# Ten slots instead of eight for the gathered expert rows of a two-layer trunk, in the room of two kept tiles

## The reference, cut to what matters

```python
for i in range(2):
    h = h + token_mixer(rms_norm(h, ...))          # three kinds of attention, then y @ w_o[i]
    h = h + peer_ffn(rms_norm(h, ...))             # product-key experts
    h = h + per_layer_embedding(h, p[i], ...)      # sigmoid(norm(h) @ w_ple_gate) * (p_i @ w_ple)
return rms_norm(h, final_norm_g)

def peer_ffn(h):                                   # for each token
    scores = queries x sub_keys                    # 8 heads, two halves, 128 keys
    s1, i1 = top_k(scores half 0, 16); s2, i2 = top_k(scores half 1, 16)
    top_s, top_j = top_k(s1 + s2, 16); ids = i1 * 128 + i2 at top_j
    act = softmax(top_s) * gelu(expert_u[ids] . x)
    out = sum over heads and k of act * expert_v[ids]
```

## Time and profile before

| what | value |
|---|---|
| median of 3 runs | 1553.22 us (1552.20 to 1555.97) |
| the profiled execution, own time | 1551.98 us |
| its span, first to last instruction | 1550.2 us |
| mean granted TensorE clock | 0.803 of full speed |
| read from HBM | 605.09 MB, 391 GB/s over the span |

### The profile page before, as it was taken

The page is one execution under the profiler, slowest core; times in us unless marked ns, Lnnn a source line. Parts: engine busy times, 40 slices in busy tenths (PEclk is TensorE's granted clock), DMA queues, the critical chain, the costliest instruction groups (busy, mean ns, idle before and its releaser), DMA issues.

```text
span 1550.2 us, 18373 instructions
## 1 busy us (share of the span) xinstructions
PE 1140.1 (74%) x6360; PEld 446.3 (29%) x6360; DVE 1071.2 (69%) x2731; ACT 574.1 (37%) x1800; POOL 577.8 (37%) x516
## 2 busy tenths in 40 slices
PE   9987676895558865688657887698565866777666
PEld 6754133351113522235112343245011311111112
DVE  3489996579997245567998536757799664454455
ACT  0514456333343135423334325733234443333332
POOL 0023544445443232435453323434344343333330
PEclk9999788987779976789678897889657986656668
DMA  9178999999999999999999999999999999999993
GB/s 360 61 286 343 417 411 402 375 412 422 420 411 417 418 416 419 420 418 397 422 421 418 420 418 414 398 390 419 419 421 422 400 422 421 422 421 422 421 421 117
DMA packets 90254, 607.36 MB, mean 392 GB/s; under 512 B 9904, under 2 KB 10416, under 8 KB 24624
## 3 DMA queue, kind: packets, MB, share of 16 engines
q0 software_dynamic: 73728, 536.90, 84.1%
q1 hardware_dynamic: 16272, 69.02, 11.2%
q10 hardware_dynamic: 160, 0.26, 0.1%
HBM read 605.09 MB, written 1.05 MB: 391 GB/s over the span
## 4 chain that ended last, share of the span: by engine, by line
DVE 32%; DMA 31%; PE 26%; ACT 5%; issue 4%; POOL 2%; DVEq 0%; POOLq 0%; ACTq 0%
DMA ring<-in_rows,ids 31%; DVE ring L1272 14%; PE acc L572 8%; PE bank L868 2%; PE bank L724 2%; PE bank L605 2%; POOL ring L539 2%; DVE wb L1567 2%; PE bank L950 2%; PE bank L640 1%; DVE top_i L1561 1%; DVE y L1640 1%; PE bank L610 1%; DVE top_i L1576 1%; DVE y L1576 1%
## 5 line engine op out<-in xcount | busy, mean ns | idle before, releaser
L539 POOL DMA_INDIRECT ring<-in_rows,ids x512 | 577.6, 1128 | 931.8 <-PE acc L572 769.0
L572 PE MATMUL acc<-ring,diag 64*64 64x512 f32 x3968 | 682.0, 797 | 320.3 <-ACT diag L1038 316.1
L1272 DVE CUSTOM_DVE_ANT_0 ring<-ring,xc 128x1024 f32<-128x1024 f32 x504 | 606.6, 1224 | 359.0 <-DMA ring<-in_rows,ids 352.9
L1029 ACT ACTIVATE gel<-pre 128x1 f32<-128x1 f32 x512 | 103.3, 202 | 792.0 <-DVE pre L1272 765.7
L572 PEld LDWEIGHTS acc<-ring,diag 64*64 64x64 f32 x3968 | 139.5, 160 | 807.2 <-ACT diag L1038 690.3
L1038 ACT ACTIVATE diag<-cst,act_w 128x64 f32<-128x64 f32 x512 | 178.0, 348 | 17.1
L1035 ACT ACTIVATE act_w<-gate,gel 128x1 f32<-128x1 f32 x512 | 150.7, 294 | 17.1
L724 PE MATMUL bank<-wring,hT 128*128 128x512 f32 x96 | 47.1, 636 | 4.8 <-DVE hT L1309 4.1
L868 PE MATMUL bank<-hT,held 128*128 128x128 f32 x384 | 46.1, 278 | 3.1 <-DVE hT L1306 3.1
L868 PEld LDWEIGHTS bank<-hT,held 128*128 128x128 f32 x384 | 43.8, 192 | 13.0 <-issue 7.3
L1272 DVE DVE_READ_ACCUMULATOR2_ANT pre<- 128x1 f32 x512 | 41.7, 81 | 0.0
(11 more groups left out here) (278 smaller groups left out, 1103.1 us busy)
## 6 DMA issues: line engine op xcount, KB each, us to landing
wring<-in_w_in SPq DMA_DIRECT2D x16, 978.0 KB
wring<-in_w_out SPq DMA_DIRECT2D x12, 1024.0 KB
wring<-in_w_gate SPq DMA_DIRECT2D x11, 1024.0 KB
held<-in_w_query SPq DMA_DIRECT2D x8, 1024.0 KB, 16.3
ring<-in_rows,ids POOLq DMA_INDIRECT x512
ring<-in_w_in SPq DMA_DIRECT2D x8, 978.0 KB, 14.3
held<-in_w_out SPq DMA_DIRECT2D x2, 1024.0 KB, 12.1
held_latent<-in_w_latent SPq DMA_DIRECT2D x2, 768.0 KB
```

Source lines behind the costliest of these rows:

```text
L539: pool.indirect_dma_start(out=ring[:, n % RING, :], out_offset=None, in_=rows, in_offset=bass.IndirectOffsetOnAxis(ap=index, axis=0),).the ...
L572: last = pe.matmul(acc[rows_of(c), r, :], diag[rows_of(r), j, :], ring[rows_of(r), j, D:][:, cols_of(c)], start=False, stop=True, skip_gro ...
L1029: act.activation(gel[:, j:j + 1], pre[:, j:j + 1], ACT.Gelu).then_inc(gelued, 1)
L1272: dve.tensor_tensor_reduce(out=u, in0=u, in1=x, scale=1.0, scalar=0.0, op0=ALU.mult, op1=ALU.add, accum_out=pre[:, j:j + 1]).then_inc(dott ...
```

## The change

`ring` gets ten slots. The 16 KB per partition for the two new ones come from two places. `held` has four slabs: slab 3 of `w_o` goes through `wring` in every step, so it is loaded four times, not twice. `lifts` is gone: layer 0's product p @ `w_ple` is made at the start of `embed` as in layer 1, from `w_ple` that passes through `wring` once per tile, and DVE reads it in PSUM. A small tile `p0` holds one tile's half of p, and is loaded twice. The lists of the top keys are kept for two heads at a time, not for eight.

```diff
-RING = 8
+RING = 10
-HELD = KT // 2 + 1
+HELD = KT // 2
-OUT_HELD = KT // 2 - 1
-REST_LOADS = [("out", k) for k in range(OUT_HELD)]
+REST_LOADS = [("out", k) for k in range(KT // 2)]
 def weight_order():
-    order = [(kind, k, 0) for kind, k in REST_LOADS] + [("ple", 0, 0)]
+    order = [(kind, k, 0) for kind, k in REST_LOADS]
     for w in range(STEPS):
         if w >= 1:
+            order += [("ple", 0, w - 1)] if w <= TILES else []
             order += [(kind, k, w - 1) for kind, k in EMBED_LOADS
...
-        lifts = sb("lifts", [P, TILES, D])
+        p0 = sb("p0", [P, 2, P])
-        top_v = sb("top_v", [P, 2 * PH, TOPK])
-        top_i = sb("top_i", [P, 2 * PH, TOPK], U32)
+        top_v = sb("top_v", [P, 4, TOPK])
+        top_i = sb("top_i", [P, 4, TOPK], U32)
...
                 if n == WRING:
-                    load(slab(HELD - 1), source["out"](0, OUT_HELD), held_in[HELD - 1])
-                    for i in range(HELD - 1):
+                    for i in range(HELD):
                         load(slab(i), source["query"](0, i), held_in[i])
                     load(held_keys[:], source["keys"](0, 0), held_keys_in)
-                    load_p(0)
+                    load_p0(0)
+                if (kind, k, s) == ("gate", 2, 0):
+                    load_p0(1)
...
                 if (kind, k, s) == ("out", 0, TILES):
-                    load(slab(HELD - 1), source["out"](1, OUT_HELD), held_in[HELD - 1])
...
                 if n < RING:
-                    pool.wait_ge(slab_used, n + 1)
+                    pool.wait_ge(slab_used, min(n + 1, KT))
...
             def project_out(s, k):
-                kept = k == OUT_HELD
-                w = held[:, HELD - 1, :] if kept else weights()
+                w = weights()
...
-                    if kept:
+                    if k == KT // 2 - 1 and c == 0:
                         last.then_inc(out_half, 1)
-                if not kept:
-                    release(last)
+                release(last)
...
             def rest(s, turn):          # PE
                 if s == 1:
-                    next_of(lift_copied, 2)
...
             def choose(s, c, turn):     # PE
-                    if (s, c, i) == (0, 2, 4):
-                        pe.wait_ge(pT_in[0], 16)
-                        products(0, 0, weights(), bank[2:4]).then_inc(lift_made, 1)
-                    if (s, c, i) == (0, 3, 3):
-                        next_of(lift_copied, 2)
-                        release(products(0, 1, weights(), bank[2:4]))
...
             def lift(s):                # PE, at the start of embed
                 if l == 0:
+                    next_of(pT_in[0], 16)
+                    release(products(p0, weights()))
                     return
...
             def choose(s, c, turn):     # ACT
-                if (s, c) in ((0, 2), (0, 3)):
-                    for half in range(2):
-                        act.activation(lifts[:, c - 2, half * 512:(half + 1) * 512], bank[2 + half][:, :],
-                                       ACT.Copy).then_inc(lift_copied, 1)
...
                     for c in range(2):  # DVE, rest
-                        if i == 2:
+                        if i == 2 and c == 0:
                             next_of(out_half)
+                        if i == 2 and c == 1:
+                            wait_products(dve, "out", s, KT // 2 - 1)
...
-                    link(dve.tensor_tensor(g, g, made, ALU.mult))
+                    link(dve.tensor_tensor(g, g, bank[4 + c][:, :], ALU.mult))
```

More of the change, by code:

```diff
@@ L275, in trunk @@
         best_i = part_i[:, 1]
-        pT = (lifts[:, 1, 0:2 * SEQ].rearrange("p (a s) -> p a s", a=2), kTf[:])
+        p1 = kTf[:]
         hT_next = xc[:, 1, :].rearrange("p (k c) -> p k c", k=KT)
-        xc_tail = (xc[:, 0, :], lifts[:, 0, :])
-        gain_tail = lifts[:, 1, 0:512]
+        xc_tail = (xc[:, 0, :], held[:, 2, 0:D])
+        gain_tail = held[:, 2, D:D + 512]
         h_tail = wa[:, 0:1024].rearrange("p (r n) -> p r n", r=2)
@@ L325, in trunk @@
         lift_read = sem("lift_read")
-        lift_made = sem("lift_made")
-        lift_copied = sem("lift_copied")
         latent_done = sem("latent_done")
@@ L467, in slab, with load_p0 @@
                 return held[:, i, :].rearrange("p (a n) -> p a n", a=2)
-            def load_p(l):
-                load(pT[l], p_t[l * 2 * P:(l + 1) * 2 * P, :].rearrange("(a p) s -> p a s", p=P), pT_in[l])
+            def load_p0(t):
+                load(p0[:], p_t[0:2 * P, t * P:(t + 1) * P].rearrange("(a p) s -> p a s", p=P), pT_in[0])
             for n, (kind, k, s) in enumerate(order):
@@ L493, in _ @@
                 if (kind, k, s) == ("out", 2, TILES):
-                    for i in range(2, HELD - 1):
+                    for i in range(2, HELD):
                         load(slab(i), source["query"](1, i), held_in[i])
@@ L498, in _ @@
                     sp.wait_ge(query_ready, len(CHUNKS[0]) + 2 * (STEPS - 1))
-                    load_p(1)
+                    load(p1, p_t[2 * P:4 * P, :].rearrange("(a p) s -> p a s", p=P), pT_in[1])
                     load(slab(0), source["ple"](l, 0), held_in[0])
@@ L715, in project_out @@
                 l, t = layer_tile(s)
-                kept = k == OUT_HELD
-                if kept and t == 0:
-                    next_of(held_in[HELD - 1], 16)
-                w = held[:, HELD - 1, :] if kept else weights()
+                w = weights()
                 g = min(k, 2)
@@ L886, in rest, with products @@
                 turn()
-            def products(l, t, w, b):
+            def products(p, w):
                 for c in range(2):
                     for k in range(2):
-                        last = pe.matmul(b[c][:, :], pT[l][:, k, t * P:(t + 1) * P],
+                        last = pe.matmul(bank[4 + c][:, :], p[:, k, :],
                                          w[:, k * D + c * 512:k * D + c * 512 + 512], start=(k == 0), stop=(k == 1))
@@ L926, in lift @@
                     pe.wait_ge(pT_in[1], 16)
-                if s < STEPS - 1:
-                    products(l, t, held[:, 0, :], bank[4:6])
+                    products(p1[:, :, 0:P], held[:, 0, :])
                     return
@@ L934, in lift @@
                         for c in range(2):
-                            pe.matmul(bank[4 + r][rows_of(c), :], pT[l][:, k, tokens],
+                            pe.matmul(bank[4 + r][rows_of(c), :], p1[:, k, tokens],
                                       held[:, 0, :][:, k * D + c * 512:k * D + c * 512 + 512],
@@ L945, in embed @@
                 turn()
-                if l == DEPTH - 1 and s < STEPS - 1:
+                if s < STEPS - 1:
                     lift(s)
@@ L1583, in keys_top8 @@
                     next_of(keys_half)
-                top8(range(2 * a, 2 * z), top_v, top_i, lambda i: score(i, s))
+                first = 2 * a % 4
+                top8(range(first, first + 2 * (z - a)), top_v, top_i, lambda i: score(2 * a - first + i, s))
             def keys_next8(s, c):
+                a, z = CHUNKS[s][c]
+                first = 2 * a % 4
                 def spare(i):
-                    return wb[:, (2 * work_slot(i // 2, s) + i % 2) * P:(2 * work_slot(i // 2, s) + i % 2 + 1) * P]
-                a, z = CHUNKS[s][c]
-                next8(range(2 * a, 2 * z), top_v, top_i, lambda i: score(i, s), spare, s == 0)
+                    n = 2 * work_slot(a + (i - first) // 2, s) + i % 2
+                    return wb[:, n * P:(n + 1) * P]
+                next8(range(first, first + 2 * (z - a)), top_v, top_i, lambda i: score(2 * a - first + i, s), spare, s == 0)
             def choose(s, c, turn):
@@ L1603, in choose @@
                 turn()
-                halves = slice(2 * h0, 2 * (h0 + n))
+                halves = slice(2 * h0 % 4, 2 * h0 % 4 + 2 * n)
                 link(dve.tensor_copy(top_f[:, halves], top_i[:, halves]))
```

## The result

The changed kernel takes 1563.19 us (median of 5 runs, 1561.82 to 1567.07) against 1553.22. The ratio of the runs is 1.0061, 95% interval 1.0045 to 1.0076: 9.5 us slower, 7.0 to 11.8. The forecast was 5 us faster, with a range that ended at 1560.

What follows compares the result with a forecast made beforehand. The kernel was taken as bound by bytes at a 421 GB/s plateau. Slots -18.3, reloads +7.5 and start +5.5 gave -5.3 us against 1551.98: 1546.7, and 1548 for the runs' median, range 1540 to 1560.

Steps and rivals of the forecast that it cites:

- What two more slots give: Between first and last rows, two more slots keep the DMA engines running 5.0 us longer per stall: 18.3 us won.
- the first stall: 124 to 160 us, 7.7 us lost; two rows lying ready before the wait at 224.8 us win back 5.0.
- Reloads, 7.5 us: Three more slabs, two of `w_o` and one of `w_ple`, 3.15 MB in the bound stretch: 7.5 us lost, from 5.
- The start, 5.5 us, bounds 4.4 and 8.0: Step 0: slab 3 lands at 87.0 us behind queries, keys and p; PE waits, first rows come 5.5 us late.
- The reloads' landing in later steps: Slab 3 after step 0: a slab takes 7.3 us, 12.8 us are available in step 1, so cost nothing.
- the embedding product: Moved to the start of `embed` of steps 0 and 1, about 3.7 us each, covered by the deeper ring: 0.
- the text had said would make it wrong: Signs against the prediction: the plateau moves, stalls keep their size, or PE waits for `wring` after the start.
- The third, depth unused: Rival: stalls end with the compute engines, only some 6 us won of 13.0 lost; 7 us slower, 1560; chance 0.20.
- Its threshold: The depth-unused rival decides from the point where the two slots win less than 13.0 us.
- The rival with the start hidden: Slab 3 lands earlier than in order: 5.5 us better than the sum, 1542; 0.17 together with all rate back.

Runs made afterwards that it cites:

- reloads at eight slots: The changed kernel with slab 3 of step 0 issued first, as before the change, and `RING = 8`: 1565.23 us, 1.0074 against the kernel before.
- the run with thin loads: Ten slots, slab 3 first, the three added loads cut to an eighth of their columns (output not the reference's): 1549.62 us, 0.9975 against the kernel before.
- the new shares: Expert-row shares in the attention part of steps 1 and 3 raised by a fifth: 1552.78 us on ten slots with gates first, 1561.24 us on the kernel before.
- the two experiments: Slab 3 issued first again in the changed kernel: 1555.22 us; kept slab 3 issued behind queries, keys and p in the kernel before: 1560.55 us.
- the gates first: Changed kernel with slab 3 first, second p load later, `w_ple` behind the gate slabs and its product behind the gate products: 1556.69 us, 1.0018 against the kernel before.
- nine slots: The ten-slot kernel with the gates first, given `RING = 9` and slab 3 kept in `held`: 1552.82 us, 0.9997 against the kernel before.

## Why the prediction was wrong, by its own steps

**The failed step is "What two more slots give".** It had 18.3 us, with bounds of 9 and 25. Measured, it is 9.3 us with the reloads in place (0.60%; the intervals of the two kernels, some 0.25% and 0.13% on either side, leave about 4 us to each side). At nearly the bytes of before it is some 4.9 us (2.9 to 6.6 by that run's interval), below the lower bound. The sum after the fact, in ratios against the kernel before: reloads at eight slots +0.74% (11.5 us), two slots -0.60% (9.3 us), the late start +0.47% (7.3 us), together +0.61%. It closes by construction, since each term is a difference of neighbours. The same difference can be split the other way, through the run with thin loads: two slots -4.9 us, bytes 7.0, the late start 7.3. Between the two prices of the slots lie 4 us, which the reloads cost with eight slots beyond their bytes.

The step gave every stall a reserve of 5.0 us of its own, "if the engines have waited for rows in between". Waits for rows do lie in between, but they lay beside a dense chain that is nearly as long. When the rows came early, DVE waited for ACT and the next dense instruction was no earlier, as the lines at 237.9 and 246.5 us show. From the first row to the end of step 1's attention the dense chain sets the time once there are eight slots, with a fixed number of rows. Ten slots against eight change that time by 1.0 us, and the 63 rows not at all. The slots let two more rows lie ready at its end, and that is one reserve for all of it: 5.6 us are won by the 81st row, where the step had counted 5.0 at the first stall, 4.1 at 272 and a share of 1.9 at 236. Step 3 has a chain of the same kind, and the second gain, from 7.7 to 10.4 us, comes behind it.

More rows in the chain are another matter. With the new shares and ten slots it takes 182.9 us with 66 rows: three rows more, 7.5 us of bytes, for 3.6 us. With the new shares and eight slots it takes 189.5 us. So the old order fixed too few rows for ten slots, and the new one too many for eight.

The evidence for a reserve in the first stall was misread, too. The 11.1 us at 224.8 us are a row's transfer, as the chain follows it back, and not the wait of an engine. DVE waited 4.1 us there, in four pieces, and no wait of DVE for a row in the whole trace is longer than 3.9 us.

**Reloads, 7.5 us: right in bytes, short in effect.** The price per byte held (6.1 us for 6.5). But with eight slots the reloads cost 11.5 us (interval 7.8 to 15.4). Some 4 us are then more than the bytes, though the interval's lower end is only just above 7.5. Part of what the slots bring only repairs what making room for them did, as far as those 4 us are real. Which of the reloads' waits make it up was not separated and stays open.

**The start, 5.5 us, bounds 4.4 and 8.0: right in mechanism, small.** The landing at 87.0 came at 87.1. The product ran at 1.2 GHz nearly throughout (6.70 us) and cost 6.2 us at the first row; 6.2 and 7.3 us in the two experiments. The query product behind it took 2.05 us, not 3.42, so 1.4 us came back, as the text had reckoned. The 5.5 us were thus too low for the product alone: with it at 1.2 GHz throughout, as the row with the clock of 0.50 after a gap suggested, 8.0 less 1.4 is 6.6 us.

**The reloads' landing in later steps, and the embedding product, at 0: the costs hold, their working does not.** The 7.3 us are the distance between the landings of two queued slabs, and not the time of one from issue to landing, which is 12.4 us in the same rows. A gate slab took 15.7 and 11.1 us, and PE waited for it, as the text had said would make it wrong. Removing the waits for gate slabs changed nothing that could be measured with ten slots.

**The rivals.** The third, depth unused, gave 1560 and came nearest. (Its own rows, the stalls of 272 and 1012, give 6.8 us won, where it says some 6.) Its threshold, 13.0 us to be won, was right in kind: 9.3 lay below it. Its place was only half right: not DVE alone in the first stall, but the chain of PE, ACT and DVE up to the end of the attention. The rival with the start hidden is refuted: both experiments carried it whole.

## What to carry to other kernels

A deeper buffer did not shorten a dense part whose order is fixed; it left one reserve to be used behind it. So count one reserve for each such part and not one for each stall, and before adding stalls up, ask at each wait for data what dense instruction comes next, and when its other inputs are ready. A list of shares that was tuned for one depth must be tuned again for another: ten slots with the old shares lost 0.18%, the same kernel with new shares came even, and the new shares with eight slots lost 0.59%. A transfer in the chain that ended last is not a wait of that length: look at what the engine itself waited. When a load changes from one buffer to another, look first where its issue now stands in the queue: one moved line was worth 6 us, as much as all the bytes.

No version here with the right output beats the kernel before. The best are even with it: ten slots with the gates first and the new shares (0.9993), and nine slots (0.9997, with the new shares 0.9995).

## What the runs showed of the hardware

A small load beside the row queue can cost more than its bytes. In the changed kernel 0.13 MB of p, in pieces of 512 B, stands right ahead of a gate slab:

```profile
p<-in_p_t SPq DMA_DIRECT2D x1, 128.0 KB, 9.3
```

It landed 9.3 us after its issue and the slab 15.7 us after its own; without p ahead the slab took 11.1 us. So p cost the slab 4.6 us of latency; at 421 GB/s its bytes are 0.3 us. The Trainium skill ("DMA: Bandwidth & Descriptors", section "Queues, rings and completion order") has each engine go round between queues packet by packet; by that a short packet would wait for a row's packet just as a long one does. The 4.6 us are in line with it, but no run separates this from other causes, and it is not the same everywhere. Before the change, p of layer 1, 0.26 MB in pieces of 1 KB, landed sooner,

```profile
kTf<-in_p_t SPq DMA_DIRECT2D x1, 256.0 KB, 5.7
```

and the 1.05 MB slab behind it 12.4 us after its own issue.

The rate where nothing but rows runs is 421 GB/s with six, eight and ten rows of 1 MB in flight. What depth changes is the time beside the dense work, and there the worth of a slot falls steeply: 46 us each from six to eight, at the bytes of before. From eight to ten it is some 4.9 us for both at nearly those bytes, and 9.3 us for both with the reloads in place.
